# Three projection groups of a hybrid recurrent layer ahead of two others, on one Trainium2 core

## The reference

```
h = rms(x) * (1 + scale) + shift
proj = h @ w_in                     # all branches' inputs in one projection
A: gated DeltaNet   q, k, v by a causal conv of 4; chunks of 64 tokens,
                    a unit triangular solve in each; state S carried over chunks
B: HGRN2            q, f, i; logf by log-sigmoid of f, cumulated in a chunk;
                    scores with a decay per channel; state carried over chunks
C: Mamba-2 SSD      x, B, C by a causal conv of 4; decays; state carried
D: mLSTM            q, k, v; decays with a running maximum; state carried
y = (sum over branches of sigmoid(gate) * (branch @ w_branch)) @ w_out
x = x + gate * y;   then norm, SwiGLU of width 2816, residual, final norm
```

## Time and profile before

| | us |
|---|---|
| median of 3 runs | 1176.51 (1175.53 to 1179.0) |
| profiled execution | 1176.42 |
| its span | 1174.6 |
| TensorE busy | 1101.2 (94%) |
| VectorE busy | 820.2 (70%) |
| ScalarE busy | 458.2 (39%) |
| DMA | 116.99 MB, mean 100 GB/s |

### The profile page before, as it was taken

One profiled execution on the slowest core, in us unless ns is written; L12 is line 12 of the kernel. 1 busy time (PEld: TensorE's weight loads), 2 busy tenths in 40 slices (PEclk: granted clock), 3 DMA queues, 4 the chain that ended last, 5 costly groups with the idle time before them and its releaser, 6 DMA issues.

```text
span 1174.6 us, 26651 instructions
## 1 busy us (share of the span) xinstructions
PE 1101.2 (94%) x11347; PEld 1029.5 (88%) x11347; DVE 820.2 (70%) x1464; ACT 458.2 (39%) x686; POOL 11.6 (1%) x29
## 2 busy tenths in 40 slices
PE   5889979999999999789999999979999999999997
PEld 3589978887667888789999999969999999999997
DVE  1647967778667865678888885586888889763433
ACT  2534495721102315763343332145444434541121
POOL 0001100000000000000000000000000000000000
PEclk9889999999869989989999999989999999999999
DMA  9924421112557216113333334222233333233201
GB/s 302 273 80 102 101 73 38 38 39 83 157 161 211 83 38 166 39 37 73 99 101 101 104 99 149 73 72 73 73 107 84 98 109 97 79 105 90 87 14 77
DMA packets 191052, 116.99 MB, mean 100 GB/s; under 512 B 36650, under 2 KB 189351, under 8 KB 190678
## 3 DMA queue, kind: packets, MB, share of 16 engines
q1 hardware_dynamic: 190358, 115.16, 34.7%
q0 software_dynamic: 576, 0.14, 0.1%
HBM read 108.31 MB, written 6.96 MB: 98 GB/s over the span
## 4 chain that ended last, share of the span: by engine, by line
PE 71%; DVE 6%; ACT 2%; issue 1%; DVEq 1%; ACTq 1%; PEldq 0%; PEld 0%
PE ps L924 70%; PE ps L928 1%; DVEq L2294 1%; DVE scr_parts L2992 1%; DVE pj L2274 1%; DVE pj_parts L3300 1%; ACTq L2123 0%; DVE scr L2706 0%; ACT rstd L1879 0%; DVE scr L2778 0%; DVE Vr L3254 0%; ACT scr_parts L2069 0%; DVEq L2275 0%; DVE scr L2953 0%; ACT scr L1989 0%
## 5 line engine op out<-in xcount | busy, mean ns | idle before, releaser
L924 PE MATMUL ps<-high_parts,scr_parts 128*128 128x272 f32 x1396 | 315.8, 297 | 22.4 <-DVE scr_parts L2992 9.5
L924 PE MATMUL ps<-hT_parts,scr_parts 128*128 128x272 f32 x960 | 263.3, 294 | 1.2 <-DVE pj_parts L3300 1.2
L924 PEld LDWEIGHTS ps<-high_parts,scr_parts 128*128 128x128 f32 x1396 | 239.4, 195 | 25.2 <-issue 12.7
L924 PE MATMUL ps<-pj_parts,scr_parts 128*128 128x272 f32 x1560 | 249.0, 289 | 0.3 <-issue 0.3
L924 PE MATMUL ps<-high_parts,ring_parts 128*128 128x272 f32 x812 | 238.6, 294 | 0.0
L924 PEld LDWEIGHTS ps<-pj_parts,scr_parts 128*128 128x128 f32 x1560 | 217.1, 188 | 0.7 <-issue 0.7
L924 PEld LDWEIGHTS ps<-hT_parts,scr_parts 128*128 128x128 f32 x960 | 179.1, 193 | 1.4 <-DVE scr_parts L2992 1.4
L924 PEld LDWEIGHTS ps<-high_parts,ring_parts 128*128 128x128 f32 x812 | 157.8, 194 | 0.7
L2992 DVE TENSOR_TENSOR scr_parts<-ring,scr_parts 128x1024 fp32r<-128x1024 f32 (+1 forms) x38 | 52.7, 1392 | 84.2 <-ACT scr_parts L2016 83.0
L2016 ACT ACTIVATE scr_parts<-ring 128x1024 fp32r<-128x1024 f32 (+1 forms) x38 | 44.9, 1191 | 142.6 <-PE ps L924 142.5
L924 PE MATMUL ps<-scr 64*64 64x64 f32 (+6 forms) x2352 | 80.4, 233 | 3.1 <-DVEq L2294 1.9
(11 more groups left out here) (424 smaller groups left out, 1820.3 us busy)
## 6 DMA issues: line engine op xcount, KB each, us to landing
ring<-in_w_in_dram SPq DMA_DIRECT2D x62, 512.0 KB, 5.1
ring<-in_ffn_w_in_dram SPq DMA_DIRECT2D x44, 512.0 KB, 5.2
ring<-in_ada_w_dram SPq DMA_DIRECT2D x40, 512.0 KB, 5.9
ring<-in_ffn_w_out_dram SPq DMA_DIRECT2D x16, 384.0 KB, 3.5
ring<-in_ffn_w_out_dram SPq DMA_DIRECT2D x16, 320.0 KB, 4.2
pj<-in_ada_w_dram SPq DMA_DIRECT2D x8, 512.0 KB, 8.3
ring<-in_w_out_dram SPq DMA_DIRECT2D x8, 512.0 KB, 4.2
x_scratch<-scr SPq DMA_DIRECT2D x1, 2176.0 KB, 12.2
```

What stands on the lines that cost most here:

```text
L924: return pe.matmul(out, lhsT, rhs, start=start, stop=stop, skip_group_check=True)
```

## The change

Only `MIX_ORDER` is changed. HGRN2's groups 4, 5, 6 stand ahead of the state-space branch's 9, 10. So the loads' column offsets, the features that an eviction writes and the numbers that `units_through` gives change with it, and `shared_order` computes a new list for all engines. Costs, `NEEDS`, `SEQUENCE` and the constants of SyncE's queue are as they were.

```diff
-MIX_ORDER = [0, 1, 2, 9, 10, 4, 5, 6, 11, 12, 13]
+MIX_ORDER = [0, 1, 2, 4, 5, 6, 9, 10, 11, 12, 13]
 EARLY = 2 * len(MIX_ORDER)
 MIX_ORDER += [8, 14]
```

## The result

The changed kernel takes 1212.72 us (1211.71 to 1217.66, 4 runs) against 1176.02 us: ratio 1.0311, 95% interval 1.0267 to 1.0355. It is slower by 37 us. The forecast was slower by 12, in a range that ended at 1204.

What follows compares the result with a forecast made beforehand. TensorE was taken as nearly full with three chains' small matmuls, ScalarE bounding 146 to 175 us. The late shared chain (451) plus 4 for ScalarE ends the mixing stage at 455, not 443: 1176.4 + 12 = 1188 us, range 1166 to 1204.

Steps and rivals of the forecast that it cites:

- SyncE's wait at a cost of 0: SyncE's queue before modulation unit 4: sample state ready at 333.5, load lands at 351, slack of 17.5 us used up, cost 0.
- The rival with this wait: Shared chain keeps its present pace, unit 4's weights come 17 us late and TensorE waits: 1205 us, chance 0.16.
- the other waits of the queue: SyncE's waits for GDN's and HGRN2's states were to come no later than now.
- The late shared chain: State-space then mLSTM tiles start 60.1 us later, run near the fastest intervals, end last at 455 instead of 434.0.
- the 7 us off: Shared chain, up to its first exponential: 7 us less waiting behind GDN's inverse square roots on ScalarE.
- HGRN2 done at 396: HGRN2 starts behind tile 11, 43.5 us earlier, and at the same pace ends at 396 instead of 439.2.
- ScalarE's crowd: ScalarE from 146 to about 205 us: HGRN2's preparation beside GDN's square roots, net 14 us more work, delaying tile 15 by 4.
- The 17 loads of function tables: ScalarE's table loads for GDN's square roots and HGRN2's preparation: 22 us by the trace, 45 by the skill's figure.
- The faster rival: HGRN2 and GDN fill ScalarE's waits, state-space tiles move into 285 to 381 us at a higher clock: 1168 us, chance 0.29.

Runs made afterwards that it cites:

- e1: The changed kernel with SyncE's wait for the state-space sample state moved from load 23 to load 30 (SSD_OUT = 30): 1194.05 us, ratio 1.0158.
- e3: Old group order, but the shared chain's first projection-fed step is planned only behind tile 15; HGRN2 not early; SSD_OUT = 30: 1211.53 us, ratio 1.0305.
- e4: Changed kernel's order with only one HGRN2 group (4) ahead of the state-space branch's two, SSD_OUT = 30: 1197.61 us, ratio 1.0195.
- e5: Changed kernel, SSD_OUT still 23, planner places modulation unit 4's second half and later units only 15 us behind the sample state: 1198.14 us, ratio 1.0186.
- e6: Changed kernel's order with two HGRN2 groups (4, 5) ahead of the state-space branch's two, SSD_OUT = 30: 1195.76 us, ratio 1.0156.
- e10: e1 laid out again with the planner's WEIGHT 0.002 instead of 0.003: 1206.52 us, ratio 1.0249.
- e11: e3 laid out again with the planner's WEIGHT 0.002 instead of 0.003: 1217.19 us, ratio 1.0335.
- e8: e1 with the planner preferring the shared chain by 0.3 us in each choice: 1210.11 us, ratio 1.03.
- e2: The kernel before, old group order, with SyncE's wait for the sample state moved from load 23 to load 30: 1179.16 us, ratio 1.0022.
- e7: The kernel before with the planner's WEIGHT 0.01 instead of 0.003: 1180.07 us, ratio 1.0022.
- e9: The kernel before with the planner's margin for fillers, FILL, 0.3 instead of 0.7: 1182.27 us, ratio 1.0028.

## Why the prediction was wrong

**The step that failed: SyncE's wait at a cost of 0.** "The load goes out at 345 and lands 5.9 us later, at 351. TensorE used it at 350.7." The first half was too late, the second wrong. The sample state came at 324.8, not 333.5, and load 24 went out at 333.0 and was in use at 338.6. But TensorE came to the weights at 330.2, not at 350.7. I took the time of need from the trace of before, though all fillers move: with the shared chain absent from 175 to 228 us, tiles take its place (the last early one 28 us sooner), and the modulation units begin sooner too. The rival with this wait had 16% and a price of 17 us; the wait measured 18.7 us (e1). That the two are so near is luck: the rival had TensorE stand for 17 us, and it stood for 9. Forecast plus rival, 1205, still lay below 1212.7. The prediction also said that the other waits of the queue come no later than before. GDN's comes 10 us later (L779 at 359.8 instead of 350.1), and in the experiments that moved the first wait, this second one held loads back.

**The price of a stall.** TensorE waited for the weights only 9 us (8.4 and 0.7), but moving the wait won 18.7. The two profiled executions run the same list of work and their stages differ by 21.8 us: 9.2 are idle time and 12.6 are the same matmuls taking longer (365.5 against 352.9). e1 has 0.73 as its clock from 300 to 375 us, the new order 0.56, against 0.81 before. So with the stall the clock was also lower for the matmuls behind it. The prediction had no such term; it counted the clock only where it could be won. The Trainium skill ("TensorE: Matmul & The Clock Gate", section "HAM oscillation — how this bites in real kernels") describes a kernel in which each wait for a transfer leaves the matmuls behind it at the lower clock. Here the trace agrees in direction: 0.57 and 0.50 in the stretches with and behind the wait. The wait is not the only reason, for the kernel before is at 0.65 from 325 to 350 us with 1.1 us of idle time.

**The late shared chain: the number near, in part by luck.** It was to end at 455 and end last. Without SyncE's wait at load 23 it ended at 460.6 and last; 17 us over before measured (e1), 12 forecast. These are its exponentials in e1, behind tile 15's eviction at 187.95:

```profile
226.04 0.62 ACT L1989 ACTIVATE scr<-scr 128x512 f32<-128x512 f32 x1
...
299.76 0.42 ACT L1989 ACTIVATE scr<-scr 32x256 f32<-32x256 f32 x1 [0.68 <-DVEq L2294]
...
332.71 0.41 ACT L1989 ACTIVATE scr<-scr 128x256 f32<-128x256 f32 x1
...
440.14 0.31 ACT L1989 ACTIVATE scr<-scr 32x128 f32<-32x128 f32 x1 [1.78 <-DVE scr L2568]
```

The terms of the sum, forecast and then e1: tile 15 at 198 (188.0); to the first exponential 37.2, with the 7 us off (38.1); four state-space intervals 76.2 (73.7); to mLSTM's first 25.4 (33.0); mLSTM's four intervals 91.7 (107.4); to the end 26.6 (20.5). The state-space tiles did run at the fastest pace. The mLSTM tiles did not: they took 23 us more than forecast, close to the pace of before, and the earlier tile 15 and the shorter end hid most of it. With SyncE's wait, the sample tile to mLSTM's first took 45.5 us and mLSTM's four intervals 112.4.

Nor does the last chain alone set the end. In e3, e4, e5, e6, e10 and e11 GDN ends last (at 478.0 in e3, L2736, where it was 442.6 before), though nothing in these kernels moves its start. All three chains end late together, and hurrying one of them (e8) made the other two end later: they share TensorE, and what is lost is its time, idle or slow.

**HGRN2 done at 396: wrong.** It ended at 462.6, and at 441.8 in e1, when before it was 439.2. Starting sooner did not make it finish sooner. The likely reason is in the planner: it gives each chain's step its turn by when it can start, so HGRN2 shares the engines with the other chains for longer; no run tests this.

**What the sum can be split into.** The new order is 33.6 us over e2. 18.7 are the wait at load 23 (new order over e1), and 14.9 are all the rest (e1 over e2): the late chain, whatever the early HGRN2 gives or costs, and what SyncE's queue still takes. By e3 one could write the rest as +32.4 for the late chain and -17.5 for the early HGRN2. These figures add up by the way they are formed, and both hold the longer stalls of e3, so they are no measured terms. The remaining 3 us to the 37 are e2's difference to before, which is within the noise.

**ScalarE's crowd: no cost seen.** From 146 to 194 us ScalarE was busy 40.4 us (33.5 before) and TensorE idled 7.8 us (6.2 before), but tile 15 was out 4.1 us sooner. I had 4 us for a later tile 15. No run isolates this term: the shared chain's matmuls are gone from that stretch too. The 17 loads of function tables that I counted became 13, because steps with the same function now met (an exponential, L1942, at 163.33 with no load, right behind the exponential of L1894 at 161.25):

```profile
L1944 ACT ACT_TABLE_LOAD x4 | 5.1, 1283 | 0.2
...
L1892 ACT ACT_TABLE_LOAD x2 | 2.6, 1283 | 0.0
...
L1942 ACT ACT_TABLE_LOAD x1 | 1.3, 1283 | 0.1
```

L1892 and L1942 load twice and once instead of four and three times, at 1283 ns as before.

**The faster rival.** The state-space tiles did move towards 285 to 381 us, but the clock there fell to 0.64 instead of rising, with 16.8 us of idle time. A good part of that is SyncE's wait: e1 has 0.79 and 11.7 us there. It is still worse than the 0.84 and 6.6 us before; that the tiles and units which had kept TensorE dense were used up earlier is likely (the last early tile is out 28 us sooner), but not tested.

**What stays open.** What the late chain costs and what the early HGRN2 gives back, each without a stall of SyncE's queue, is open: no kernel here has the late chain without the early HGRN2 and without such a stall. Why e4 loses 18 us for a delay of two tiles is not settled; from 75 us to the end of the stage TensorE idles 30.0 us in both e4 (390.1 - 360.2) and e6 (388.7 - 358.7), at a clock of 0.89 in both, so the rows of the stage don't tell a delay of two tiles from one of four. That a low clock follows idle time is seen in each kernel here; no run changed the clock alone.

## What to carry to other kernels

When work is laid out by a planner, a reordering moves the fillers too, so the time at which an engine will need a transfer can't be read from the old trace; ask for each wait in a hand-written queue whether the planner knows it. Moving such a wait to a later place exposes the next one, so when it is moved as a control, look for what ScalarE and TensorE wait for behind it. All orders here that let the longest chain start later lost 16 us or more, so start it first. And a gap on TensorE can cost up to twice its length: added idle time was paid 1.4 to 2.2 times in the kernels with the late chain, where the matmuls ran at a lower clock, but about once in e7 and half in e9, where the mean clock was that of before or better.

## What the runs showed of the hardware that I had not expected

With the matmuls the same, their busy time from 75 us to the end of the stage was 348.1 us at a mean clock of 0.93, 352.9 at 0.91, 363.6 at 0.88 and 365.5 at 0.87. From 350 to 375 us of the new order the granted clock was 0.50 of 2.4 GHz although the records have TensorE busy 25.0 of 25 us; before that stretch it had idled 9.1 us of 25:

```profile
325.00:350.00 25.00, 15.87 (x158) 9.50 (x157) 6.20 (x18) 2.10 (x6) 0.00 (x0) 0.57 0.88 251
350.00:375.00 25.00, 25.00 (x282) 16.53 (x282) 10.69 (x21) 0.20 (x1) 0.00 (x0) 0.50 0.37 107
375.00:400.00 25.00, 22.38 (x452) 17.51 (x448) 20.46 (x39) 7.06 (x14) 0.00 (x0) 0.95 0.66 193
```

0.50 is the lower of its two levels, 1.2 GHz, for all of these 25 us; the next stretch is back at 0.95. So a stretch that looks full can be a slow one; PEclk tells, the busy share doesn't.
